# The last RMS norm moved from a phase of its own into the tiles of the second expert layer

## The reference

```python
def hier_moe(h, wg, bg, we, be, w1, w3, w2):
    ...
    xs = hf[tok]                                   # tokens sorted by expert
    a = lax.ragged_dot(xs, w1, sizes)
    b = lax.ragged_dot(xs, w3, sizes)
    o = lax.ragged_dot(jax.nn.silu(a) * b, w2, sizes)
    o = o * wts.reshape(-1)[order][:, None].astype(o.dtype)
    y = jnp.zeros_like(hf).at[tok].add(o)          # each token gets two rows
...
        x = x + (1 + g2)[:, None, :] * hier_moe(hn, ...)
    return rmsnorm(x, final_g)                     # x * rsqrt(mean(x * x) + 1e-6) * final_g
```

## Time and profile before

| | us |
|---|---|
| median of three runs | 6346.73 |
| the profiled execution | 6351.06 |
| its span, first to last instruction | 6349.4 |
| TensorE busy in the span | 6004.5 (95%) |
| VectorE busy | 3428.8 (54%) |
| ScalarE busy | 2003.1 (32%) |
| GpSimd busy | 1669.8 (26%) |

### The profile page before, as it was taken

One profiled execution on the slowest core, in us unless ns is written; L12 is line 12 of the kernel. 1 busy time (PEld: TensorE's weight loads), 2 busy tenths in 40 slices (PEclk: granted clock), 3 DMA queues, 4 the chain that ended last, 5 costly groups with the idle time before them and its releaser, 6 DMA issues. The chain is left out here.

```text
span 6349.4 us, 84080 instructions
## 1 busy us (share of the span) xinstructions
PE 6004.5 (95%) x28942; PEld 4906.1 (77%) x28943; DVE 3428.8 (54%) x4936; ACT 2003.1 (32%) x3168; POOL 1669.8 (26%) x1525
## 2 busy tenths in 40 slices
PE   7999989999799999999979999999996999999993
PEld 5876668888578888888868888887885888888882
DVE  6889945544545545555434222224776454556554
ACT  2324422222334433444345100001113333444433
POOL 6546548720022222322200000000000222223222
PEclk9999999999899999999989999999998999999996
DMA  4655554422357666767545434443444666777766
GB/s 149 188 170 170 177 197 147 149 102 83 115 181 217 192 177 201 215 200 217 159 152 200 171 145 169 179 147 121 155 153 159 178 179 175 217 217 242 217 193 247
DMA packets 589092, 1114.30 MB, mean 175 GB/s; under 512 B 113501, under 2 KB 187325, under 8 KB 587913
## 3 DMA queue, kind: packets, MB, share of 16 engines
q1 hardware_dynamic: 411392, 821.84, 37.3%
q0 software_dynamic: 73296, 255.77, 15.8%
q10 hardware_dynamic: 104250, 34.66, 2.1%
HBM read 841.47 MB, written 270.16 MB: 175 GB/s over the span
## 5 line engine op out<-in xcount | busy, mean ns | idle before, releaser
L2157 DVE SCALAR_TENSOR_TENSOR m_o<-m_pO,m_weight_of,m_gate 128x512 f32<-128x512 f32 x320 | 239.4, 751 | 727.1 <-PE m_pO L1905 473.9
L2124 DVE TENSOR_TENSOR m_w_lo<-m_w_raw,m_w_hi 128x1024 fp32r<-128x1024 f32 x512 | 597.8, 1224 | 0.1
L139 PE MATMUL m_pA<-m_w_lo,m_xT_hi 128*128 128x512 f32 x1280 | 517.4, 404 | 8.3 <-DVE m_xT_lo L2135 8.3
L1813 POOL COPY m_gather_now<-m_gather_of 128x1 int32 (+1 forms) x164 | 185.0, 1128 | 1274.1 <-DMA x<-m_o,m_scatter_now 906.0
L1901 PE MATMUL m_pO<-m_w_lo,m_hT_hi 128*128 128x512 f32 x1280 | 512.8, 401 | 0.5 <-ACT m_hT_hi L1965 0.5
L1960 ACT ACTIVATE m_xT_hi<-m_pX 128x512 fp32r<-128x512 f32 x320 | 191.5, 599 | 1002.9 <-PE m_pB L141 994.2
L1948 ACT ACTIVATE m_w_hi<-m_w_raw 128x1024 fp32r<-128x1024 f32 x512 | 505.3, 1053 | 0.0
L141 PE MATMUL m_pA<-m_w_hi,m_xT_hi 128*128 128x512 f32 x1280 | 503.2, 393 | 0.0
L140 PE MATMUL m_pA<-m_w_hi,m_xT_lo 128*128 128x512 f32 x1280 | 500.2, 391 | 0.0
L1901 PE MATMUL m_pO<-m_w_hi,m_hT_hi 128*128 128x512 f32 x1280 | 498.9, 390 | 0.0
L139 PE MATMUL m_pB<-m_w_lo,m_xT_hi 128*128 128x512 f32 x1280 | 498.1, 389 | 0.0
(11 more groups left out here) (494 smaller groups left out, 13502.5 us busy)
## 6 DMA issues: line engine op xcount, KB each, us to landing
m_w_raw<-in_moe_w_dram SPq DMA_DIRECT2D x384, 1024.0 KB, 8.4
conv_x_hi<-hT_hi SPq DMA_DIRECT2D x24, 2048.0 KB, 8.6
conv_x_lo<-hT_lo SPq DMA_DIRECT2D x24, 2048.0 KB, 13.2
glu_ada<-in_ada_w_dram POOLq DMA_DIRECT2D x96, 256.0 KB
a_x<-in_x_dram SPq DMA_DIRECT2D x32, 512.0 KB, 3.5
a_ada<-in_ada_w_dram POOLq DMA_DIRECT2D x64, 256.0 KB, 3.4
s_u<-u SPq DMA_DIRECT2D x64, 256.0 KB, 2.8
s_r<-k SPq DMA_DIRECT2D x64, 256.0 KB
```

Source lines behind the costliest of these rows:

```text
L139: pe.matmul(out, lh, rl, start=start, stop=False)
L2124: tt(W13[s][1][:, m, k:k + 2, :], W13[s][0][:, m, k:k + 2, :], W13[s][2][:, m, k:k + 2, :].bitcast(F32), ALU.subtract).then_inc(w13_lo, 1)
L2157: dve.scalar_tensor_tensor(out=ob[:, n, :], in0=pO[:, n, :], scalar=wslot[:, bass.ds(tile_, 1)], in1=gate2[:, n, :], op0=ALU.mult, op1=ALU ...
```

## The change

`final_norm` is gone. In the second expert layer, each tile's 128 rows of x1 are fetched again after the add (`gather_y`), normalised, and stored to the output by an indirect DMA (`store_y`). A token is in two tiles, so its output row is written twice; the later one has the whole sum. To make room for the buffer `y`, the gain and `junk`, `w2_raw` keeps one half of w2 instead of two: ACT itself issues the load of the second half when the first has been split, and the split of the second half comes later in ACT's and DVE's order. The norm of tile t - 1 stands at the end of tile t on ACT and DVE. The first tile on POOL and the first two experts on ACT and DVE are written out in front of their loops.

```diff
+    RAW = 1 if final is not None else 2
...
-        w2_raw = sb("w2_raw", [P, 2, KF, HALF])
+        w2_raw = sb("w2_raw", [P, RAW, KF, HALF])
...
+        if final is not None:
+            yb, fgain, junk = sb("y", [P, D]), sb("final_gain", [P, D]), sb("junk", [P, HALF])
...
             def ahead(i, s, w13):
                 e = 2 * i + s
-                for n in range(2):
-                    sp.wait_ge(w2_lo, 4 * e + 2 * n + 2)
+                for n in range(RAW):
+                    sp.wait_ge(w2_lo, 4 * e + (4 if RAW == 1 else 2 * n + 2))
                     load_w2(e + 1, n)
...
+            def gather_y(t):
+
+                pool.wait_ge(sc_st, 16 * t + 16)
+                pool.sem_inc(ob_free, 1)
+                pool.wait_ge(normed, t + 1)
+                pool.tensor_copy(sy[:], gidx[:, bass.ds(t, 1)]).then_inc(yi_ready, 1)
+                pool.wait_ge(yi_ready, t + 1)
+                pool.sem_inc(y_gath, 1)
+                pool.indirect_dma_start(yb[:], None, x1_dram, bass.IndirectOffsetOnAxis(ap=sy[:, 0:1], axis=0)).then_inc(y_ld, 16)
+
+            def store_y(t):
+
+                pool.wait_ge(normed, t + 1)
+                pool.sem_inc(y_scat, 1)
+                pool.indirect_dma_start(out_dram, bass.IndirectOffsetOnAxis(ap=sy[:, 0:1], axis=0), yb[:], None).then_inc(out_st, 16)
+
+            def add_rows(t):
+                pool.wait_ge(o_out, 2 * t + 4)
...
+                gather(3, 3)
+                add_rows(0)
+                gather_y(0)
...
+                with pool.Fori(1, last) as t:
+                    gather(t + 3, t + 3)
+                    add_rows(t)
+                    store_y(t)
+                    pool.wait_ge(out_st, 16 * t)
+                    gather_y(t)
+                add_rows(last)
+                store_y(last)
+                pool.wait_ge(out_st, 16 * last)
+                gather_y(last)
+                store_y(last + 1)
+                pool.wait_ge(out_st, 16 * last + 16)
...
+                if RAW == 1 and n == 0:
+                    act.wait_ge(w2_lo, 4 * e + 2)
+                    act.dma_start(w2_raw[:, 0, :, :], of(w2_view, e)[1]).then_inc(w2_ld[1], 16)
+
+            def norm(m):
+
+                if final is None or isinstance(m, int) and m == 0:
+                    return
+                act.wait_ge(y_ld, 16 * m)
+                for h_ in range(2):
+                    act.activation(junk[:], yb[:, h_ * HALF:(h_ + 1) * HALF], ACT.Square, accum_out=ystat[:, h_:h_ + 1]).then_inc(y_sq, 1)
+                    act.wait_ge(y_sq, 3 * m + h_ + 1)
+                act.activation(ystat[:, 2:3], ystat[:, 1:2], ACT.Identity, scale=1.0 / D, bias=eps[:, 0:1]).then_inc(y_sq, 1)
+                act.wait_ge(y_sq, 3 * m + 3)
+                act.activation(ystat[:, 3:4], ystat[:, 0:1], ACT.Sqrt, scale=1.0 / D, bias=ystat[:, 2:3]).then_inc(y_std, 1)
...
                 silu(t + 1)
+                norm(t)
...
+            def norm(m):
+
+                if final is None or isinstance(m, int) and m == 0:
+                    return
+                dve.wait_ge(y_std, m + 1)
+                dve.reciprocal(ystat[:, 4:5], ystat[:, 3:4]).then_inc(y_rec, 1)
+                dve.wait_ge(y_rec, m + 1)
+                dve.scalar_tensor_tensor(out=yb[:], in0=yb[:], scalar=ystat[:, 4:5], in1=fgain[:],
+                                         op0=ALU.mult, op1=ALU.mult).then_inc(normed, 1)
...
                 out(t, 0)
                 out(t, 1)
+                norm(t)
...
-        core.phase(moe, ident, "m1", 1, routes, table, *experts)
-        core.phase(final_norm, "final", x1, final_g.rearrange("(a d) -> a d", a=1), out)
+        core.phase(moe, ident, "m1", 1, routes, table, *experts, final=(final_g.rearrange("(a d) -> a d", a=1), out.rearrange("b n d -> (b n) d")))
```

More of the change, by code:

```diff
@@ L1675, in _, with moe @@
             batch_ranks(NT // BT - 1)
-def moe(core, ident, tag, layer, routes, table, w1, w3, w2, mod_dram, hn_dram, x1_dram, partial=None, next_w=None):
+def moe(core, ident, tag, layer, routes, table, w1, w3, w2, mod_dram, hn_dram, x1_dram, partial=None, next_w=None, final=None):
     nc = core.nc
@@ L1808, in _ @@
                 c(pool.memset(one[:], 1.0))
+            if final is not None:
+                c(pool.memset(eps[:], EPS))
             pool.sem_inc(ob_free, 1)
@@ L1832, in _ @@
             gather(2, 2)
[L1833 to L1837, removed]
+            if final is None:
+                n = pool.value_load(table[0:1, 2 * NE:2 * NE + 1], min_val=NE, max_val=TILES)
+                with pool.Fori(0, n - 1) as t:
+                    gather(t + 3, t + 3)
+                    scatter(t)
+                scatter(n - 1)
+            else:
+                gather(3, 3)
+                add_rows(0)
+                gather_y(0)
+                last = nc.s_assert_within(first_tile(pool, NE - 1, NE - 1) + more_tiles(pool, NE - 1), NE - 1, TILES - 1,
+                                          skip_runtime_bounds_check_because="no choice of experts fills more than TILES tiles")
+                with pool.Fori(1, last) as t:
+                    gather(t + 3, t + 3)
+                    add_rows(t)
[8 more added lines that the diff above has]
+                pool.wait_ge(out_st, 16 * last + 16)
         @block.tensor
@@ L1970, in silu @@
                 act.activation(h[:], pA[:], ACT.Silu).then_inc(sil, 1)
+            if final is not None:
+                act.sem_inc(y_sq, 3)
+                act.sem_inc(y_std, 1)
             def tile(t):
@@ L2018, in section @@
                 e = 2 * i + s
-                t0, rest = first_tile(act, e), more_tiles(act, e)
+                t0, rest = first_tile(act, e) if not (isinstance(e, int) and e == 0) else 0, more_tiles(act, e)
                 first_tile_of(t0, e, (e + 1, 1 - s, at(i, s, 1)[0]))
@@ L2023, in section @@
                         tile(t0 + 1 + j)
-            with act.Fori(0, NE // 2 - 1) as i:
+            if final is not None:
+                section(0, 0)
+                section(0, 1)
+            with act.Fori(0 if final is None else 1, NE // 2 - 1) as i:
                 section(i, 0)
@@ L2035, in _ @@
             h_high(t0 + rest)
+            norm(t0 + rest)
+            norm(t0 + rest + 1)
             if next_w is not None:
@@ L2118, in _ @@
             dve.wait_ge(gate_ld, 16)
+            if final is not None:
+                dve.wait_ge(fgain_ld, 16)
             c(ts(gate2[:], gate2[:], 1.0, None, ALU.add))
@@ L2190, in _ @@
                     x_low(0, 1)
+            if final is not None:
+                dve.sem_inc(y_rec, 1)
+                dve.sem_inc(normed, 1)
             def section(i, s):
                 e = 2 * i + s
-                t0, rest = first_tile(dve, e), more_tiles(dve, e)
+                t0, rest = first_tile(dve, e) if not (isinstance(e, int) and e == 0) else 0, more_tiles(dve, e)
                 first_tile_of(t0, e, 1 - s)
@@ L2198, in section @@
                         tile(t0 + 1 + j)
-            with dve.Fori(0, NE // 2 - 1) as i:
+            if final is not None:
+                section(0, 0)
+                section(0, 1)
+            with dve.Fori(0 if final is None else 1, NE // 2 - 1) as i:
                 section(i, 0)
```

100 lines of the change are left out of this document (33 added, 67 removed).

## The result

The changed kernel takes **6719.91 us** (median of four runs, 6719.44 to 6725.41) against 6346.53 on the same chip: ratio 1.0589, interval 1.0576 to 1.0601. The forecast was 6705, range 6500 to 6860.

The account below looks back on a forecast made before the run. It took TensorE as the bound, without slack at 17.7 us a tile, with POOL's chain close behind at 16.1. Two-tile growth +409, the 14 further tiles +27 and the removed phase -74 made +362: 6705 us, range 6500 to 6860.

Parts of the forecast that it names:

- The removed phase: After the last output half: 100.6 us without matmuls replaced by 27 us, a gain of 74 us, within some 10.
- POOL's additions: On POOL, each tile: a y gather's copy, pause and issue, 2.0 us, and a wait for the store's landing, 2.2.
- The norm's pieces: From the y gather's issue: landing 3.5 us, ACT 3.5, DVE's reciprocal and product 1.5, 8.5 in all.
- The first tile: Each expert's first tile, counted from the end of DVE's norm to the next store: 27.0 us, 9.3 more than before.
- The later tile: An expert's later tiles: POOL's turn 17.4 us without weight loads, plus 0.4 and small waits, 18.1 us.
- closes a second ring over the same tile: Norm from the y gather's issue to the next store, 8.5 us, beside POOL's own 8.1; charged 0.4 us.
- The w2 order: In an expert's first tile: ACT loads w2's second half after the first is split; issue 2.3 us, landing 8.4 later.
- The clock: TensorE behind a first tile's gap: 48 matmuls could take 22 us instead of 11 at 1.2 GHz; put at 0.
- rival C: Contention and clock: lower clock in first tiles, 198 us, or loaded landings in every tile, 155; about 6880 us, chance 0.13.
- A: Rival: only POOL's ring counts, the w2 order hides behind it; 21.5 us a tile, 6566 us, chance 0.17.
- B: Rival: only the first tile's chain counts, the ring closes in 17.7 us; 6403 us, chance 0.10.
- D: Rival: only the removed phase counts, all additions under 0.95 us a tile; 6273 us, chance 0.05.

Follow-up runs that it names:

- e3: The changed kernel without the output store in the loop and its wait, only the last tile stored, output incomplete: 6650.1 us.
- e2: The changed kernel, but POOL no longer waits in the loop's gather for x's rows to land, only before its next index copy: 6708.0 us.
- e9: The changed kernel with the norm one tile later on ACT and DVE, behind x high and x low, POOL's landing wait kept: 6539.4 us.
- e1: The kernel before, norm phase kept, with one raw half of w2 in the second expert layer, ACT issuing the second half's load: 6398.8 us.
- e6: The changed kernel with SyncE instead of ACT issuing the load of w2's second half: 6692.1 us.
- e8: The changed kernel with the norm one tile later, behind x high and x low, and without POOL's wait for x's landing behind its gather: 6421.5 us.
- e11: e8 with SyncE instead of ACT issuing the load of w2's second half: 6392.1 us.
- e4: The changed kernel with 16 unread 128x128 identity matmuls ahead of the a part, to keep TensorE at work: 6736.1 us.
- e5: The changed kernel without the norm's work on ACT and DVE, rows stored as fetched, output not normalised: 6510.5 us.
- e7: The changed kernel with Identity in place of the norm's root, so ACT never changes its table, output scale wrong: 6686.6 us.

## Why the prediction was right, and which step of it was not

The time, the sign and the size of an expert came out: two tiles 48.6 forecast and 48.5 measured, three tiles 66.7 (48.6 + 18.1) and 68.0. Step by step:

- **The removed phase.** 27 us forecast for what is left, 31.8 measured. Two pieces were short: in front of the last scatter POOL waits 3.41 us for the y gather before it (3.7 us to the scatter's issue, where 1.6 was counted), and from the last store's start to the end of the program it is 10.2 us (6707.64 to 6717.8), where 6.0 was counted. ACT's last norm took 2.2 us and not 3.5, as no table is loaded there, which hid part of it.
- **POOL's additions.** The y gather's copy, pause and issue are 2.04 us as forecast. The store's landing was put at 2.2; e3, read by the ring over two tiles, makes it about 1.8.
- **The norm's pieces.** ACT 3.4 and DVE 1.5 us, as forecast. y's landing was put at 3.5: from the end of its issue it was 3.3 in 66 of the 78 tiles (mean) and 6.7 in the other 12, among them the one shown.
- **The first tile.** 27.0 forecast, 26.7 measured, and up to the end of the a part's first half two errors cancel (9.6 us behind DVE's norm by the forecast, 10.1 measured): ACT's issue costs 0.40 us and not 2.3 (the price came from SyncE's row "4.64 x2", which runs from the first start to the last end with the wait between them; a lone issue of SyncE, shown below, takes 0.38), while the first half of the a part ran at the lower clock and took 5.3 us where 2.8 was counted.
- **The later tile: the step that failed.** It said that the norm "closes a second ring over the same tile", in which the norm only has to be ready for the next store, beside 8.1 us of POOL's work; so it charged 0.4 us for it, and let POOL's own turn of 17.4 set the pace. The runs show the reverse. POOL's landing wait gives 12 us (e2). The norm's place ahead of the next x low gives 181 (e9), since it makes TensorE wait for two landings, a gather and the norm. The forecast had used just this order for the first tile (it counted "from the end of DVE's norm") and not asked the same of the tile behind. That the size came out is luck: a later tile takes 21.0 us by a ring that the forecast did not have, and the forecast reached 21.6 in a two-tile expert by another (18.1, for the most part POOL's turn, and 3.5 for the loads).
- **The w2 order.** As a chain of its own it costs 51 us (e1), 10 of them in the last expert. Giving the issue to SyncE gave 28 us in the changed kernel (e6) and 29 in e8 (e11); in e1 it was not tried. The forecast's 27.0 us lumps this chain with the norm that stands ahead of it and gave it no price of its own; and it put the last expert at nothing, in which ACT waited 12.6 us for the second half.
- **The clock.** Put at 0, with up to 198 us in rival C. It fell in the layer from 1.00 to 0.91. The estimate beside e4, some 0.7 us a later tile, is not 0 and far from C's; no run separates it.
- **The rivals.** A (6566) would have had POOL's ring alone; it is the second bound, seen once the norm is gone (e5, 6510). B is out, since the later tiles grew as well (21.0 us a tile against 17.7), and so is D: all additions together are 5.6 us a tile (437 / 78), against D's 0.95. C's landings at the loaded price in every tile did not come: the scatter's took 8.6 us (mean) in 30 of 78 tiles, about once an expert as the forecast had it, and 4.7 in the others.
- **Slips of the working.** Between DVE's first and last instruction of the first tile lie 17 operations, not 14; rival B takes 8.8 us for a norm whose pieces make 8.5; ACT's chain ends at 21.5 and not 21.3. None of them moves a sum by more than 10 us.
- **What was to be seen.** The wait of the a part for x low and the 46 to 50 us came; so did POOL's wait for the store (77 times) and the table loads. TensorE's busy share is 0.81 instead of three quarters, since part of it is matmuls at the lower clock. POOL waited for PE or DVE 7.6 us in a first tile (mean of 32) and 0.4 in a later one, well under the 3 us that would have refuted the forecast. So this sign did not tell the two rings apart, since the one over two tiles runs through POOL as well.

## What to carry to other kernels

In a loop like this one, work that waits for a round trip through memory should stand, in each engine's order, behind what feeds the busiest engine. It is not enough that the work fits into the engine's idle time: ask which instruction of the next tile is written behind it. Here the same work one tile later gave back 181 of 373 us.

Where two rings pass through one loop, an edit on the shorter one can measure as next to nothing. Test it again after the longer one is cut: the landing wait went from 12 to 118 us.

A filler that is to keep an engine at work needs its own price first: e4's took 3.7 us in every tile, also where there was no gap.

## What the runs showed of the hardware

- The issue of a 1 MB load takes 0.40 us on ACT and as little on SyncE. A row that joins several instructions hides this, since its time holds the waits between them. SyncE's issues in the changed kernel (start, us, line), and one row of e6, where two issues are joined and the second waits until both halves are split:

```profile
5247.65 0.38 SPq L1776 DMA_DIRECT2D m_w_raw<-in_moe_w_dram  x1
5265.50 12.53 SPq L1773 DMA_DIRECT2D m_w_raw<-in_moe_w_dram  x4
5315.34 0.37 SPq L1776 DMA_DIRECT2D m_w_raw<-in_moe_w_dram  x1
```

```profile
5302.07 12.36 SPq L1776 DMA_DIRECT2D m_w_raw<-in_moe_w_dram  x2
```

- Matmuls of 128x512 came 0.43 us apart behind a wait of 5.44 us, and 0.23 apart six us later, in the same product.
- From the start of a store of 128 rows by index to POOL's next copy it took 5.7 us in the tile shown, with the scatter before it in the same queue, yet taking the store out (e3) gave 0.9 us a tile.
- The y gather (128 rows, 512 KB) landed 3.3 us after the end of its issue in 66 of 78 tiles (mean) and 6.7 us after it in 12, one of them beside four weight loads; the scatter with add took 4.7 us in 48 tiles and 8.6 in 30.
- A table load took 1.28 us, 152 times (195 us of ACT), and the kernel without them was 33 us faster (e7).
